# One mixture-of-experts block in two layers: token-major closing stage in layer 1, a token's expert rows side by side in DRAM

## The chip, the core and the metric

The kernel runs on one core of a Trainium2 chip. The metric is the device time in microseconds; the time shown is the median of three runs. The profile comes from one profiled execution, whose span stands a little below the time that it took.

## What is computed

Two layers of a hybrid token mixer and a mixture of experts over 512 latent and 256 context tokens of width D = 1024, all in float32. The second half of a layer and the last norm are what the change touches:

```python
def moe_ffn(h, router_w, router_b, e_gate, e_up, e_down, s_gate, s_up, s_down):
    scores = jax.nn.sigmoid((h @ router_w).astype(jnp.float32))
    _, idx = lax.top_k(scores + router_b.astype(jnp.float32), TOP_K)      # 6 of 64
    w = jnp.take_along_axis(scores, idx, axis=-1)
    w = (w / jnp.sum(w, axis=-1, keepdims=True) * ROUTED_SCALE).astype(h.dtype)
    return routed_experts(h, idx, w, e_gate, e_up, e_down) + swiglu(h, s_gate, s_up, s_down)
...
xl = xl + g1 * yl                                  # token mixer, gated
out = moe_ffn(hl2, ...)
xl = xl + g2 * out.reshape(b, n_lat, d)            # g2: one number per channel
...
return rms_norm(xl, final_norm_w)                  # after layer 1, latent tokens only
```

Layer 0 handles 768 tokens (six tiles of 128), layer 1 behind its mixer the 512 latent ones (four tiles).

## The kernel before

**Layout.** X, the residual stream, lies channel-major in SBUF: 128 channels on the partitions, eight chunks of channels, tokens along the free side. Nearly everything lives in one big SBUF tile, `arena`, through views, and the profile names it so. PSUM has eight banks of 128 x 512. Each engine has its own program; semaphores tie them. A table of jobs (`Plan`) gives each PSUM result its bank and says which engine reads it out ("A" for ACT, "D" for DVE); `start_job`, `ready` and `evacuated` are the waits that follow from it. A float32 product on TensorE shows as two records in the trace.

**Expert stage.** Each token goes to 6 of 64 experts. DVE, TensorE and POOL first build a table of slots (the index preparation: one-hot products, then `TG`, `TS` and `IXT`, L1926 to L1934). The work goes in blocks of 64 rows, in layer 1 with 11 blocks and eight experts to a round. Per block: POOL gathers rows from `hrows` (L2124); DVE turns them (`turn`, L1965); TensorE makes gate and up (L1062); ACT the silu (`gates`, L1442); DVE the hidden rows (`hidden`, L1972); TensorE turns those (L1070) and DVE copies them (`hidden_in`, L1977); TensorE makes the down product (L1084); ACT copies it out of PSUM into `YB` (`weighted`, L1450); POOL scatters `YB` to y in DRAM, 2 KB a row (L2132). SP streams the experts' weights, 3 MB each in two pieces (L530, L534). Partitions 0 to 63 of a down product hold channels 0 to 511 of 64 rows, partitions 64 to 127 channels 512 to 1023.

**y in DRAM.** Row (k, token, half), 512 numbers, lies at `(k * 1024 + token) * 2 + half`, k being which of the token's six experts made it.

**Closing stage of a layer.** SP waits for all scatters and then reads y back, a tile of 128 tokens in two halves of channels (L630), into a ring of three tiles, `Y6`; tile t waits until tile t - 3 is used. Meanwhile TensorE makes the shared expert's down products (L704, jobs `sd`) and DVE adds them to X, gated (`shared_added`, L1953). ACT scales three of a token's six rows (`weighted_rows`, L1475), DVE adds the other three, scaled (`sums`, L2027), TensorE turns and adds the three sums (L1128, jobs `ct`, 12 products over 128 columns a half), and DVE adds the result to X with the gate (`gated`, L2015). In layer 1 the last norm follows tile by tile: ACT squares (L1499), TensorE sums over channels (L1139, job `nf`), ACT takes the root (L1187), DVE the reciprocal (L1567) and eight products into H (`last_norm`, L2005), and SP stores the tile (L638) in pieces of 512 bytes, since the output is channel-major and turned on the host. In layer 0 ACT squares X for layer 1 (L1487) once tile 3 is gated.

The order in layer 1's closing is that of each engine's program:

```python
                    else:                                   # DVE, tile t, after sums(t)
                        if t:
                            last_norm(t - 1)
                        gated(t)
...
                        if t + 1 < pl.t_out:                # ACT, tile t
                            weighted_rows(t + 1)
                        for i in range(2):                  # then the squares of tile t
```

## Time and profile before

| what | value |
|---|---|
| median of 3 runs | 2374.71 us (2373.3 to 2379.6) |
| profiled execution: its time, its span | 2376.04 us, 2374.0 us |
| mean granted TensorE clock | 0.967 |
| busy share of the span: PE, DVE, ACT, POOL | 92%, 38%, 24%, 29% |
| chain that ended last, by engine | PE 73%, DMA 14%, DVE 8%, ACT 2% |
| transfers of y to SBUF (L630) | 20 of 1536 KB |
| expert loop of layer 0, of layer 1 | 675 to 1257 us, 1764 to 2310 us |
| closing stage of layer 0, of layer 1 | from 1257 us, 2310 to 2374 us |

A row of the timeline reads: start, duration, engine, line of the kernel, operation, output<-input, shape, count of the instructions merged into it, and in brackets the engine's idle time ahead of it with what ended that. Shares of busy time are averages over stages with different limits; what a change is worth is read in the stage that it touches. Where a DMA ends a wait, the DMA share of that window (1.00 and a little over is full) says whether more could have been moved.

### The profile page before, as it was taken

The page shows a single profiled execution, that of the slowest core. Times are in us where ns is not written, and L with a number is a line of the kernel's source. Part 1 is how long each engine was busy: PE and PEld are TensorE (multiplying, and loading weights), DVE is VectorE, ACT ScalarE, POOL GpSimd, SP SyncE. Part 2 cuts the span into 40 slices and gives each one's busy share as a digit, 9 for nine tenths or more (in the row PEclk, how much of TensorE's full clock was granted, in tenths as well). Part 3 has the DMA queues.
Part 4 walks back from the last instruction along what each step waited for, and adds up shares of the span by engine and source line. Part 5 has one row for each costly group of instructions (what it writes and reads, how often), then busy time and mean ns, then how long its engine had stood idle before and what let it go on. Part 6 is the DMA issues. An engine that isn't in the chain of part 4 may idle for free.

```text
span 2374.0 us, 36610 instructions
## 1 busy us (share of the span) xinstructions
PE 2180.4 (92%) x12802; PEld 1171.5 (49%) x12802; DVE 900.5 (38%) x1851; ACT 568.8 (24%) x1175; POOL 677.6 (29%) x811
## 2 busy tenths in 40 slices
PE   5998989898899999999998898899989999999897
PEld 1474344453645555555556463354445544455446
DVE  2295676312712222222226585663352121121117
ACT  4222154313201111111113522342211111111113
POOL 0000000000335555555551000000055554555530
PEclk8999989998799999999999999999999999999999
DMA  8612000363469999999987321000269999999977
GB/s 334 238 50 75 0 1 1 124 262 129 167 272 414 418 409 407 408 417 411 410 354 274 113 84 45 1 1 18 100 239 418 417 416 411 406 412 410 413 286 248
DMA packets 104856, 594.22 MB, mean 250 GB/s; under 512 B 25142, under 2 KB 29374, under 8 KB 62528
## 3 DMA queue, kind: packets, MB, share of 16 engines
q1 hardware_dynamic: 68656, 524.73, 54.8%
q0 software_dynamic: 34672, 63.07, 7.1%
q10 hardware_dynamic: 1440, 5.24, 0.5%
q8 instruction: 55, 0.90, 0.2%
q14 instruction: 33, 0.27, 0.0%
HBM read 572.95 MB, written 60.56 MB: 267 GB/s over the span
## 4 chain that ended last, share of the span: by engine, by line
PE 73%; DMA 14%; DVE 8%; ACT 2%; issue 2%; SPq 1%; DVEq 0%; ACTq 0%; POOLq 0%
PE psum L1062 23%; PE psum L704 19%; PE psum L1084 11%; DMA arena<-in_experts 11%; PE psum L870 3%; PE psum L894 2%; PE psum L910 2%; DMA arena<-in_mod_w 2%; PE psum L782 2%; PE psum L721 2%; PE psum L808 2%; PE psum L1070 2%; DVE arena L1567 1%; DMA arena<-y 1%; PE psum L1128 1%
## 5 line engine op out<-in xcount | busy, mean ns | idle before, releaser
L1062 PE MATMUL psum<-arena 128*64 128x256 f32 x6144 | 714.8, 386 | 33.9 <-DMA arena<-in_experts 26.8
L1062 PEld LDWEIGHTS psum<-arena 128*64 128x64 f32 x6144 | 438.1, 138 | 249.5 <-issue 40.8
L704 PE MATMUL psum<-arena 128*128 128x512 f32 (+1 forms) x1360 | 513.6, 534 | 20.0 <-DVE arena L1727 7.1
L2124 POOL DMA_INDIRECT arena<-hrows,IX x384 | 393.7, 1025 | 223.7 <-POOL IX L2116 156.9
L704 PEld LDWEIGHTS psum<-arena 128*128 128x128 f32 x1360 | 260.6, 195 | 262.5 <-issue 228.1
L1084 PE MATMUL psum<-arena 128*64 128x512 f32 x1536 | 364.8, 595 | 8.8 <-DMA arena<-in_experts 7.8
L1972 DVE TENSOR_TENSOR arena<-psum,arena 128x128 f32<-128x128 f32 x192 | 56.0, 292 | 606.5 <-ACT arena L1442 606.5
L2132 POOL DMA_INDIRECT y<-arena,IX x192 | 197.2, 1027 | 303.0 <-DVE arena L1965 198.7
L1442 ACT ACTIVATE arena<-psum 128x128 f32<-128x128 f32 x192 | 53.3, 278 | 673.1 <-PE psum L1062 673.1
L1450 ACT ACTIVATE arena<-psum 128x512 f32<-128x512 f32 x192 | 114.7, 597 | 312.1 <-PE psum L1084 312.1
L1084 PEld LDWEIGHTS psum<-arena 128*64 128x64 f32 x1536 | 112.4, 137 | 145.9 <-issue 120.9
L1977 DVE COPY arena<-psum 128x128 f32<-128x128 f32 x192 | 56.0, 292 | 271.9 <-PE psum L1070 271.9
L2083 POOL TENSOR_SCALAR arena<-con,arena 1x288 f32<-1x288 f32 x2 | 2.6, 1293 | 533.6 <-DVE arena L1858 533.6
L2074 POOL COPY arena<-arena 32x4608 f32<-32x4608 f32 x2 | 8.0, 4021 | 495.9 <-PE psum L808 495.9
L1965 DVE STREAM_TRANSPOSE arena<-arena 128x512 f32<-128x512 f32 x192 | 135.3, 705 | 11.3 <-DMA arena<-hrows,IX 7.1
L870 PE MATMUL psum<-arena 96*128 96x256 f32 (+1 forms) x288 | 104.1, 481 | 3.1 <-issue 3.1
L1070 PEld LDWEIGHTS psum<-con,arena 128*128 128x128 f32 x192 | 26.6, 139 | 157.8 <-issue 157.8
L1645 DVE SCALAR_TENSOR_TENSOR arena<-arena,par 128x512 f32<-128x512 f32 (+1 forms) x180 | 103.4, 650 | 0.0
L1349 ACT ACTIVATE arena<-psum,nm 128x768 f32<-128x768 f32 (+1 forms) x80 | 65.3, 816 | 112.1 <-DVE nm L1750 112.1
L1749 DVE TENSOR_REDUCE mx<-psum 128x1 f32<-128x768 f32 (+1 forms) x80 | 67.9, 849 | 34.8 <-PE psum L870 33.8
L910 PE MATMUL psum<-con,arena 128*128 128x128 f32 x416 | 62.3, 282 | 16.9 <-ACT arena L1370 9.4
L910 PEld LDWEIGHTS psum<-con,arena 128*128 128x128 f32 x416 | 44.9, 142 | 61.7 <-issue 34.5
(253 smaller groups left out, 1753.9 us busy)
## 6 DMA issues: line engine op xcount, KB each, us to landing
arena<-in_experts SPq DMA_DIRECT2D x128, 2048.0 KB, 19.1
arena<-in_experts SPq DMA_DIRECT2D x128, 1024.0 KB, 21.9
arena<-in_mod_w SPq DMA_DIRECT2D x48, 1024.0 KB, 8.1
arena<-y SPq DMA_DIRECT2D x20, 1536.0 KB, 15.4
arena<-in_wblk SPq DMA_DIRECT2D x22, 1024.0 KB, 4.9
arena<-in_shared SPq DMA_DIRECT2D x2, 3072.0 KB, 11.8
arena<-hrows,IX POOLq DMA_INDIRECT x384, 8.1
hrows<-arena ACTq DMA_DIRECT2D x10, 512.0 KB, 2.6
```

The source lines that it names most:

```text
L704: last = mm(job(l, key, n, parts), a, b, start=i == 0, stop=i == len(pairs) - 1)
L870: last = mm(flat[:, u % 2, i * LAT:i * LAT + n], QALL[0:QK, h, qt * P:(qt + 1) * P], KALL[0:QK, h, a:a + n], start=True, stop=True)
L910: last = nc.tensor.transpose(psum[:, bk, at * P:(at + 1) * P], PR[:, u % 2, i * P:(i + 1) * P], ident)
L1062: last = mm(psum[j * ROWS:(j + 1) * ROWS, (0, 1, 5)[u], 0:2 * P], HT[:, u, k, :], w[:, k * 512 + j * 256:k * 512 + (j + 1) * 256], start=k ...
L1070: nc.tensor.transpose(psum[:, 2, 0:P], HB[:, tour.third(s), :], ident).then_inc(sem(f"hid_T{l}"), 1)
L1084: last = mm(psum[q * ROWS:(q + 1) * ROWS, (3, 4, 6)[u], :], AT[:, u, j * ROWS:(j + 1) * ROWS], w[:, 4096 + j * D + q * 512:4096 + j * D + ...
L1450: f(YB[:, r, :], psum[:, (3, 4, 6)[tour.third(s)], :], ACT.Copy).then_inc(sem(f"y_a{l}"), 1)
L1645: op = V.scalar_tensor_tensor(dst, src, w, dst, ALU.mult, ALU.add)
L1749: link(V.reduce_max(mx[:, q], flat[:, u % 2, 0:n], AX))
L1965: V.transpose(HT[:, tour.third(s), :, :].rearrange("p k (t c) -> p t k c", t=2), GR[:, r, :]).then_inc(sem(f"turned{l}"), 1)
L2124: g.indirect_dma_start(GR[:, r, h * 256:(h + 1) * 256], None, rows, offsets(IX[:, s, h:h + 1]), bounds_check=4 * T * P - 1, oob_is_err=Fal ...
L2132: g.indirect_dma_start(y6d[l], offsets(IX[:, s, 2:3]), YB[:, r, :], None, bounds_check=TOPK * STRIDE * 2 - 1, oob_is_err=False).then_inc(s ...
```

## The change

1. **y's layout, both layers.** Row (token, half, k) now lies at `(token * 2 + half) * 8 + k`. A token's six rows of a half are 12 KB in one piece, and a transfer of y has 128 pieces of 12 KB instead of 768 of 2 KB. The last step of the index preparation computes these numbers (one instruction and one link of the chain more). The ring `Y6` is ordered by half first.
2. **The gate g2 goes into the experts' rows in layer 1.** A new job `gate` (8 small products) spreads g2 over the partitions; ACT copies it to `G2`. In layer 1 `weighted` moves from ACT to DVE and multiplies by `G2` instead of copying.
3. **Closing stage of layer 1, token-major.** TensorE turns X into PSUM with products against the identity (32 over 128 columns, into all eight banks: four tiles by two halves), then adds each half's three sums there with 3 products over 512 columns (jobs `xt`). DVE adds nothing to X behind the shared expert.
4. **The last norm, token-major.** A token is a partition, so ACT squares and sums a whole tile in one instruction (128 x 1024, accumulated) and takes a 128 x 1 root; DVE takes a 128 x 1 reciprocal and makes the output in two instructions of 128 x 512 from PSUM, with the norm's weights as rows in `FW`, 512 KB that SP loads ahead of the first transfer of y.
5. **The output** is stored token-major, 4 KB a piece.

```diff
@@ Plan
-            self.shared += ["signs", ("sg", 0, 0), "eid", ("sg", 1, 0)] + oh + ["tab", "ix", ("su", 0, 0), ("su", 1, 0)]
+            self.shared += ["gate", "signs", ("sg", 0, 0), "eid", ("sg", 1, 0)] + oh + ["tab", "ix", ("su", 0, 0), ("su", 1, 0)]
...
-            j += [(("ct", t, i), "D") for i in range(2)]
-            if l == LAYERS - 1:
-                j += [(("nf", t), "A")]
+            j += [(("ct" if l == 0 else "xt", t, i), "D") for i in range(2)]
...
+            elif k[0] == "xt":
+                bk = 2 * k[1] + k[2]
@@ SP
+                if l == LAYERS - 1:
+                    sp.dma_start(FW, A["final"]).then_inc(sem("final_in"), 16)
                 for t in range(pl.t_out):
                     if t >= 3:
-                        ready(sp, l, ("ct", t - 3, 1))
+                        ready(sp, l, ("ct" if l == 0 else "xt", t - 3, 1))
                     for i in range(2):
-                        half = slice(i * 512, (i + 1) * 512)
-                        sp.dma_start(Y6[:, t % 3, :, half], y6d[l].rearrange("(k t p c) d -> t p k c d", k=TOPK, p=P, c=2)[t][:, :, i, :]
+                        sp.dma_start(Y6[:, t % 3, i, :, :].rearrange("p k d -> p (k d)"),
+                                     y6d[l].rearrange("(t p c q) d -> t c p (q d)", p=P, c=2, q=8)[t, i, :, 0:TOPK * 512]
                                      ).then_inc(sem(f"y6in{t % 3}{i}"), 16)
...
-                sp.wait_ge(sem(f"norm_used{l}"), pl.norm[("nf", t)] + 1)
-                sp.dma_start(out[:, :, t * P:(t + 1) * P], H[:, :, t * P:(t + 1) * P]).then_inc(sem("out_done"), 16)
+                evacuated(sp, l, ("xt", t, 1))
+                sp.dma_start(out[t * P:(t + 1) * P, :], O[t]).then_inc(sem("out_done"), 16)
@@ TensorE
+                    elif st == "gate":
+                        start_job(st)
+                        for m in range(KC):
+                            q = m // 4
+                            last = mm(psum[q * ROWS:(q + 1) * ROWS, pl.bank[st], (m % 4) * P:(m % 4 + 1) * P],
+                                      modTs[l][:, 5 * KC + m, 0:1].to_broadcast([P, ROWS]), ident, start=True, stop=True)
+                        last.then_inc(done, 1)
...
+                if l == LAYERS - 1:
+                    evacuated(pe, l, ("sd", KC - 1, 0))
+                    for t in range(pl.t_out):
+                        for i in range(2):
+                            start_job(("xt", t, i))
+                            for k in range(4):
+                                mm(job(l, ("xt", t, i))[:, k * P:(k + 1) * P], X[:, 4 * i + k, t * P:(t + 1) * P], ident,
+                                   start=k == 0, stop=False)
+                    for t in range(pl.t_out):
+                        for i in range(2):
+                            pe.wait_ge(sem(f"ysum{l}"), 2 * t + i + 1)
+                            for y in range(3):
+                                last = mm(job(l, ("xt", t, i)), ident, Y6[:, t % 3, i, y, :], start=False, stop=y == 2)
+                            last.then_inc(done, 1)
@@ ACT
+                    elif st == "gate":
+                        ready(act, l, st)
+                        f(G2[:, :], job(l, st), ACT.Copy).then_inc(evacA, 1)
...
-                        weighted(s, i)
+                        if l == 0:
+                            weighted(s, i)
...
-                        for i in range(2):
-                            evacuated(act, l, ("ct", t, i))
...
-                        root(("nf", t), P)
+                        ready(act, l, ("xt", t, 1))
+                        f(JUNK, psum[:, 2 * t:2 * t + 2, :].rearrange("p b n -> p (b n)"), ACT.Square, accum_out=ssq[:, t:t + 1]
+                          ).then_inc(sem("sum_made"), 1)
+                        act.wait_ge(sem("sum_made"), t + 1)
+                        f(rms[:, t:t + 1], ssq[:, t:t + 1], ACT.Sqrt, bias=epsb[:, 0:1], scale=1.0 / D).then_inc(sem("rms"), 1)
@@ DVE
-                link(V.tensor_scalar(TS, job(l, "ix", 3 * SUBS)[:, 2 * SUBS:3 * SUBS], c("half"), None, ALU.add))
+                link(V.tensor_scalar(TS, job(l, "ix", 3 * SUBS)[:, 2 * SUBS:3 * SUBS], 0.5, -1.0, ALU.mult, ALU.add))
...
+                V.tensor_scalar(TU, TS, STRIDE - 1, 4, ALU.bitwise_and, ALU.logical_shift_left)
+                link(V.tensor_scalar(TS, TS, 10, None, ALU.arith_shift_right))
+                V.scalar_tensor_tensor(ixt[:, :, 2, :], TS.rearrange("p (h j) -> p h j", h=2), c("half"), TU.rearrange("p (h j) -> p h j", h=2),
+                                       ALU.add, ALU.add
...
+                def weighted(s, i):
+                    dve.wait_ge(sem(f"down{l}"), i * n + (s + 1))
+                    r, u = tour.place(s, tour.y_ring)
+                    dve.wait_ge(sem(f"scat{r}_{l}"), i * 16 * tour.uses(r, tour.y_ring) + (16 * u + scat0))
+                    dve.sem_inc(sem("passed"), 1)
+                    V.tensor_tensor(YB[:, r, :], psum[:, (3, 4, 6)[tour.third(s)], :], G2[:, :], ALU.mult).then_inc(sem(f"y_a{l}"), 1)
...
                             hidden(ahead, i * n + (s + 1))
+                        if l:
+                            weighted(s, i)
+                        if not (last_round and ahead == 0):
                             hidden_in(ahead, i * n + (s + 1))
...
                 def last_norm(t):
-                    r = recip(("nf", t), P)
-                    for k in range(KC):
-                        last = V.scalar_tensor_tensor(H[:, k, t * P:(t + 1) * P], X[:, k, t * P:(t + 1) * P], pr(l, "final", k), r,
-                                                      ALU.mult, ALU.mult)
-                    last.then_inc(norm_used, 1)
+                    dve.wait_ge(sem("rms"), t + 1)
+                    link(V.reciprocal(rms[:, t:t + 1], rms[:, t:t + 1]))
+                    if t == 0:
+                        dve.wait_ge(sem("final_in"), 16)
+                    for i in range(2):
+                        V.scalar_tensor_tensor(O[t][:, i * 512:(i + 1) * 512], job(l, ("xt", t, i)), rms[:, t:t + 1],
+                                               FW[:, i * 512:(i + 1) * 512], ALU.mult, ALU.mult).then_inc(evacD, 1)
...
-                    else:
-                        if t:
-                            last_norm(t - 1)
-                        gated(t)
-                evacuated(dve, l, ("ct", T - 1, 1))
+                    elif t:
+                        last_norm(t - 1)
```

**Where the order moves.** Line numbers of the changed kernel are its own. TensorE at the end of layer 1, from the last block's turned hidden rows on, before:

```order
L1070 MATMUL psum<-con,arena 128x128
L1084 MATMUL psum<-arena 64x512 x4
L704 MATMUL psum<-arena 128x512 x16
L1128 MATMUL psum<-con,arena 128x128 x24
L1139 MATMUL psum<-arena,con 128x128 x8
```

and now, L1133 being the products that carry X into PSUM and L1139 those that add the sums of y:

```order
L1084 MATMUL psum<-con,arena 128x128
L1098 MATMUL psum<-arena 64x512 x4
L711 MATMUL psum<-arena 128x512 x16
L1133 MATMUL psum<-con,arena 128x128 x32
L1139 MATMUL psum<-arena,con 128x512 x24
```

Before, the last two rows came once for each of the four tiles; now all 32 products of X stand ahead of the 24 that need y.

ACT at the same place, from the last copy of the experts' rows to the scaling of tile 2, before:

```order
L1450 ACTIVATE arena<-psum 128x512
L1475 ACTIVATE arena<-arena,WTS 128x512 x12
L1499 ACTIVATE arena<-arena 128x512 x2
L1187 ACT_TABLE_LOAD
L1187 ACTIVATE arena<-psum,epsb 128x128
L1475 ACTIVATE arena<-arena,WTS 128x512 x6
```

and now:

```order
L1461 ACTIVATE arena<-psum 128x128
L1495 ACTIVATE arena<-arena,WTS 128x512 x12
L1516 ACTIVATE arena,ssq<-psum 128x1024
L1519 ACT_TABLE_LOAD
L1519 ACTIVATE rms<-ssq,epsb 128x1
L1495 ACTIVATE arena<-arena,WTS 128x512 x6
```

The scaling of tile 2 (the last row) stands behind the square and the root of tile 0 as before, and these now wait for TensorE's products of tile 0 alone.

DVE, from the hidden rows of the last block on, before:

```order
L1972 TENSOR_TENSOR arena<-psum,arena 128x128
L1977 COPY arena<-psum 128x128
L1953 SCALAR_TENSOR_TENSOR arena<-psum,modT1,arena 128x512 x8
L2027 SCALAR_TENSOR_TENSOR arena<-arena,WTS 128x512 x6
L2015 SCALAR_TENSOR_TENSOR arena<-psum,modT1,arena 128x128 x8
```

and now, L2006 being the product with the gate row and L2062 the sums:

```order
L1993 TENSOR_TENSOR arena<-psum,arena 128x128
L2006 TENSOR_TENSOR arena<-psum,arena 128x512
L1998 COPY arena<-psum 128x128
L2004 REGISTER_ALU
L2006 TENSOR_TENSOR arena<-psum,arena 128x512
L1974 SCALAR_TENSOR_TENSOR arena<-psum,modT,arena 128x512 x8
L2062 SCALAR_TENSOR_TENSOR arena<-arena,WTS 128x512 x12
L2037 RECIPROCAL rms<-rms 128x1
L2041 SCALAR_TENSOR_TENSOR arena<-psum,rms,arena 128x512 x2
```

The gate product of a block stands between the next block's hidden rows and their copy, in every block of layer 1; in the closing the sums of tiles 0 and 1 follow each other, with nothing of tile 0 between them.

## Rows read from the trace of the kernel before

**Rows 1.** Windows: expert loops of layers 0 and 1, busy us by engine.

```profile
core 0: us, PE busy (x) PEld busy (x) DVE busy (x) ACT busy (x) POOL busy (x), PEclk, DMA share, GB/s
...
700.00:800.00 100.00, 100.00 (x738) 52.29 (x736) 21.80 (x54) 15.74 (x36) 58.90 (x72) 1.00 1.01 412
...
2190.00:2259.00 69.00, 62.98 (x453) 34.14 (x450) 13.34 (x33) 9.46 (x22) 35.77 (x45) 0.98 1.00 407
```

**Rows 2.** Timeline: layer 1's last blocks and closing stage.

```profile
2301.45 3.67 PE L1062 MATMUL psum<-arena 128*64 128x256 f32 x32
...
2307.58 1.94 PE L1084 MATMUL psum<-arena 128*64 128x512 f32 x8 [0.47 <-DVE arena L1977]
...
2310.63 13.97 PE L704 MATMUL psum<-arena 128*128 128x512 f32 x32 [1.12 <-ACT arena L1450]
...
2314.02 24.06 SPq L630 DMA_DIRECT2D arena<-y  x8
...
2324.64 0.75 DVE L1953 SCALAR_TENSOR_TENSOR arena<-psum,modT,arena 128x512 f32<-128x512 f32 x1 [0.97 <-PE psum L704]
...
2327.43 8.56 PE L1128 MATMUL psum<-con,arena 128*128 128x128 f32 x48 [2.83 <-DVE arena L2027]
...
2346.21 4.05 DVE L2027 SCALAR_TENSOR_TENSOR arena<-arena,WTS 128x512 f32<-128x512 f32 x6
...
2348.33 5.62 PE L1128 MATMUL psum<-con,arena 128*128 128x128 f32 x48 [0.16 <-DVE arena L2027]
...
2351.19 1.95 ACT L1475 ACTIVATE arena<-arena,WTS 128x512 f32<-128x512 f32 x3 [0.79 <-DMA arena<-y]
...
2353.27 2.15 DVE L2015 SCALAR_TENSOR_TENSOR arena<-psum,modT,arena 128x128 f32<-128x128 f32 x8
...
2359.31 0.95 DVE L1567 RECIPROCAL arena<-arena 128x128 f32<-128x128 f32 x1
...
2367.92 2.19 DVE L2005 SCALAR_TENSOR_TENSOR arena<-arena,par 128x128 f32<-128x128 f32 x8
```

**Rows 3.** Timeline: layer 0's closing stage.

```profile
1272.01 0.75 DVE L1953 SCALAR_TENSOR_TENSOR arena<-psum,modT,arena 128x512 f32<-128x512 f32 x1 [0.97 <-PE psum L704]
...
1278.19 3.22 DVE L1953 SCALAR_TENSOR_TENSOR arena<-psum,modT,arena 128x256 f32<-128x256 f32 x8
...
1307.27 1.95 ACT L1475 ACTIVATE arena<-arena,WTS 128x512 f32<-128x512 f32 x3 [2.12 <-DMA arena<-y]
...
1313.50 4.27 ACT L1487 ACTIVATE arena<-arena 128x512 f32<-128x512 f32 x8 [4.28 <-DVE arena L2015]
```

**Rows 4.** Windows: layer 0's closing, expert weights alone, layer 1's closing.

```profile
1295.00:1300.00 5.00, 3.65 (x30) 3.46 (x31) 4.24 (x12) 2.81 (x5) 0.00 (x0) 1.00 1.05 387
...
1745.00:1747.00 2.00, 1.68 (x30) 1.48 (x33) 0.23 (x1) 0.88 (x1) 0.00 (x0) 0.50 1.05 451
...
2328.00:2330.00 2.00, 2.00 (x12) 2.00 (x11) 0.60 (x1) 0.91 (x2) 0.00 (x0) 0.50 1.05 384
```

**Rows 5.** Instructions by form: count, busy us, mean ns, idle before.

```profile
L1450 ACT ACTIVATE arena<-psum 128x512 f32<-128x512 f32 x192 | 114.7, 597 | 312.1 <-PE psum L1084 312.1
...
L1349 ACT ACTIVATE arena<-psum,nm 128x768 f32<-128x768 f32 x64 | 57.7, 901 | 99.5 <-DVE nm L1750 99.5
...
L1802 DVE TENSOR_TENSOR arena<-psum,arena 128x512 f32<-128x512 f32 x4 | 2.8, 692 | 27.9 <-PE psum L704 26.6 <-issue 1.3
...
L1187 ACT ACT_TABLE_LOAD x5 | 6.4, 1283 | 0.1
```

**Rows 6.** Timeline: layer 1, where the gate row comes in.

```profile
1722.28 0.45 ACT L1422 ACTIVATE arena<-arena,con 128x192 f32<-128x192 f32 x1 [2.33 <-DVE arena L1858]
...
1728.25 0.81 PE L1011 MATMUL psum<-con,tot 128*1 128x128 f32 x6 [2.21 <-DVE tot L1891]
```

**Rows 7.** Timeline: layer 1 behind the index preparation.

```profile
1748.12 14.89 PE L704 MATMUL psum<-arena 128*128 128x512 f32 x32
...
1750.08 0.97 POOL L2116 COPY IX<-arena 128x3 int32 x2 [13.57 <-DVEq L1936]
...
1763.88 1.30 DVE L1965 STREAM_TRANSPOSE arena<-arena 128x512 f32<-128x512 f32 x2
```

53 lines of the change are left out of this document (22 added, 31 removed).

## The prediction

> **What bounds the kernel now.** I read four views: the windows of both expert loops, the timeline of each layer's closing stage, the windows of the same stretches, and the list of instruction forms for prices. The reader is to see three regimes.
>
> The expert loops. In layer 0 TensorE is busy 100.00 of 100 us while the DMA engines show a share of 1.01; in layer 1 TensorE is busy 62.98 of 69 us, the DMA share is 1.00 [rows 1]. Both loops therefore run at the DMA limit, and layer 1 waits for it. DVE is busy 21.8% and 19% there, ACT 16% and 14%. What the change puts on DVE in layer 1 has room; what it does to the transfers has none.
>
> The closing stage of layer 1, from the last down product to the end, 64 us. SP issues the eight transfers of y at 2314.02. ACT waits for them up to the last one, at 2351.19 (idle 0.79, released by the DMA) [rows 2]. Per tile of 128 tokens DVE works 4.05 (L2027, sums of the six rows), 2.15 (L2015, the gated addition to X), 0.95 (L1567, reciprocal) and 2.19 (L2005, final norm), 9.3 us. Two transfers take 2 x 4.07 = 8.14 us (the size and rate behind this stand below). So DVE sets the pace, and lags the last landing by 19 us: the last norm runs from 2367.92 to 2370.1, and the span ends at 2374.0 [rows 2].
>
> The closing stage of layer 0. ACT waits for y before nearly every half tile: one begins at 1307.27 after 2.12 of idle for the DMA. DVE needs only 4.1 + 2.15 = 6.3 us for a tile against 8.14 of transfer. The squares that open layer 1 start at 1313.50 [rows 3], after half (4,1). Transfers set this pace, at 387 GB/s with a share of 1.05 [rows 4].
>
> **The change, part by part.** The base is the profiled execution: span 2374.0, time 2376.0; the median of the runs is 2374.7, so I take gains off 2374.7.
>
> *Transfers of y.* A half tile is 128 x 3072 x 4 bytes = 1.573 MB, before as 768 pieces of 2 KB, now as 128 pieces of 12 KB. At 387 GB/s it takes 4.07 us. No transfer of y before has long pieces. Bounds: 387 GB/s (pieces don't matter) and 451 GB/s, the expert weights alone, whose pieces are 16 and 8 KB [rows 4]. I take 445, since the weights' row is the nearest in shape: 3.54 us, 0.53 saved.
>
> The Trainium skill (DMA: Bandwidth & Descriptors, "Why small descriptors are slow (HBM only)") states a fixed overhead of about 3 cycles for each packet beside its 32-byte beats; for 2 KB that is 3 in 67, an estimate of 4%. By it a half tile would still take 3.9 us and layer 0 would save 1.6 us where my sum has 5. The 451 against 387 GB/s of rows 4 is a larger step than that, so the trace speaks against the small figure.
>
> *Layer 0 closing.* Ten halves stand ahead of the squares: 10 x 0.53 = 5.3. Other engines cap it. DVE has shared additions up to 1272.01 + 0.75 = 1272.8 [rows 3] (the next eight begin at 1278.19 only because they stand behind the first sums), then 4.1 of sums, 3.2 of context additions, and for tiles 1 to 4 each 4.1 + 2.15, so gated tile 3 ends at 1305.7: at most 7.8 gained. And the transfers of tile 3 wait for TensorE's products of tile 0. Those follow 8 shared products over 256 columns and end at about 1284.6 (1279 + 24 x 0.234), just when the queue would run dry at 445 GB/s: a gap of at most 2 us, part of it behind DVE's own work. I take 5; bounds 0 and 7.8.
>
> *Layer 1, order.* Work falls away on DVE: 2.15, 0.95 and 2.19 a tile become a 128x1 reciprocal (about 0.2) and two 128x512 operations from PSUM (0.75 each by L1953). ACT loses two squares and a 128x128 root, gains one 128x1024 square from PSUM: 0.60 for 512 and 0.90 for 768 columns give some 1.15 [rows 5], and I allow 0.2 for reading its accumulator. TensorE: a product over 512 columns costs 13.97 / 16 = 0.873, one over 128 columns 5.62 / 24 = 0.234 (two records each) [rows 2]. So six new products a tile cost 5.24 (before 5.62 and 2.1), and 32 new ones carry X into PSUM: 7.5 us, once.
>
> Now the chain, from 2325.4, where DVE ends the last shared addition (L1953, 2324.64 + 0.75) [rows 2] and the 32 may start:
> X in PSUM 2332.9; tile 0 added 2338.1. ACT, in order, squares tile 0 (1.35), loads a table (1.28 [rows 5]), takes the root: 2341.3. Only then does it scale tile 2 (2 x 1.95): 2345.2; squares tile 1: 2347.0; scales tile 3: 2350.9. DVE's last sums and TensorE's (3,0), which holds (3,1) back by half a microsecond: products end at 2356.3. Then square 1.5 with hops, root 0.3, reciprocal 0.3, two outputs 1.6: 2360.1. The output takes 3.9 (2370.1 to 2374.0 before): 2364.0. **Gain 10.0.** The pace setter is a new one, ACT's queue behind TensorE's 7.5 us, not DVE and not y.
>
> Is y early enough? The transfers of tile 3 wait for ("xt", 0, 1), 2338.2, and land at 2343.8 and 2347.4; at 387 GB/s at 2345.9 and 2349.9. ACT takes them at 2347.0 and 2348.9, so the slow rate costs the tail 0.5 at most. FW (0.5 MB ahead of y on SP's queue) delays all landings by 1.2, hidden: the first sums wait for 2325.4 in any case. Bounds for the tail: 12.2 if ACT's order costs nothing and TensorE alone paces it (2325.4 + 7.5 + 4 x 5.24 = 2353.9, + 7.7); 7 if TensorE's clock stays low (below).
>
> *Expert loop of layer 1.* The 128x512 copy leaves ACT (0.597) and becomes a product on DVE (0.69 by the same form, L1802) [rows 5]. Behind it on DVE stands the copy of the next block's transposed hidden rows; TensorE wants that only after the next gate and up products, 3.67 us later [rows 2], so 0.69 is covered. POOL's scatter waits for it instead of for ACT: +0.1, covered. Where nothing covers it is the last block: there TensorE already waits 0.47 for that copy (L1084 at 2307.58 [rows 2]); it will wait 0.6 longer. **Loss 0.6**, bounds 0 and 1.
>
> *Gate row* (8 products of 128 columns, 1 us; one ACT copy 0.6): ahead of the signs in layer 1. TensorE waits 2.21 for the block numbers a little later, and ACT idles 2.33 just before the signs [rows 6]. Nothing; without that cover 1.6.
>
> *Index preparation*, both layers: one more shift-and-mask (0.3) and one link (0.3). POOL's first index copy goes from 1750.08 to 1750.7, while TensorE has 14.89 us of shared products from 1748.12 and DVE turns the first rows at 1763.88 [rows 7]. Nothing; layer 0 has two context passes more of the same cover.
>
> Sum: 5 + 10.0 - 0.6 = 14.4; 2374.7 - 14.4 = **2360.3**. What a measurement can tell from no change is 0.3%, 7 us.
>
> **Rivals.**
> A, the forecast, 0.55.
> B, pieces don't matter: y stays at 387 GB/s. For it: a share of 1.05 whatever the piece. Layer 0 gains nothing, the tail 9.5: 2374.7 - 9.5 + 0.6 = 2365.8. Chance 0.18.
> C, TensorE's clock. It fell to 0.50 (1.2 GHz) in 2328 to 2330 [rows 4], after 2.83 idle between the shared products and the first sums [rows 2]. With the 32 products there the idle shrinks to 2325.4 - 2324.6 = 0.8 us, so I expect the high level; at the low one for 6 us the chain starts 3 later: 2363.3. Chance 0.08.
> D, better: no gap in layer 0 (7.5) and ACT's order costs nothing (12.2), 512-byte pieces gone from the output (1): 2354.6. Chance 0.09.
> E, slower: the pitch. A token's rows now lie 32 KB apart, partition after partition, in reads and in the scatter. If lock-step streams collide, each of the 18 halves that count (10 and 8) grows. Price: 18 x 4.07 = 73 us per doubling. It decides from 13% on: 9.4 us of gain gone at 343 GB/s; by a quarter longer 2383. Against it: before, the six rows of a token lay 4 MB apart and ran at 387. The same would hit the scatters: of a round of 69 us the weights take 25.2 MB / 0.451 = 56, scatters and gathers 13; a fifth more on half of that is 1.3 us a round, eight rounds 10 us. Chance 0.06.
> The Trainium skill (DMA: Bandwidth & Descriptors, "Latency and other measured facts") names such a collision for row pitches that are large powers of two; its losses begin above 512 KiB, far over 32 KB, and no run here has shown one, so it does not raise the chance.
> F, DVE holds the loop: its product stands behind the turn of rows that may wait for a gather, so a late gather now delays scatter and PSUM release as well. Gathers are issued three blocks ahead, and a block is 3.67 + 1.94 us of products [rows 2]; a loss of 1 us a round would give 2368. Chance 0.04.
>
> **Numbers.** Likeliest 2360.3, printed as 2360. B gives 2366 and C on top of it 2368; D 2354 with a spread of 1 below. Range 2353 to 2368 leaves out E, part of F, and a little at either end, under 2 in 10. Faster by over 0.3% (below 2367.6): A, B, C, D, 0.90. Within: F and a mild E, 0.06. Slower: the rest, 0.04.
>
> **What would show it.** The windows of layer 0's closing at some 440 GB/s, not 387, and the squares of layer 1 at about 1308.5. In the tail: no 128x128 operations on DVE; 32 products from 2325 on for 7.5 us; ACT idle until tile 0's products end, then never waiting for the DMA; the last square about 15 us after the first. Rounds of layer 1 still 69 us apart and products of 0.69 on DVE. I am wrong if ACT still waits for y at the end, if the rounds lengthen, or if the tail gains under 7.

## The result, and the profile after

| | before | changed |
|---|---|---|
| median of the runs, us | 2374.97 (2369.44 to 2381.09, 8 runs) | 2358.0 (2352.49 to 2364.24, 8 runs) |
| ratio, 95% interval | | 0.9927 (0.9908 to 0.9946) |
| profiled execution, time and span, us | 2376.0, 2374.0 | 2353.7, 2352.0 |
| mean granted clock | 0.967 | 0.974 |

17.0 us faster; 14.4 were forecast. The profiled executions differ by 22.0. To see where, I cut each span at five rows that every kernel here has: the first gate product of a layer's expert loop, the last scatter of y that belongs to a block (POOL), the first squares of layer 1 (ACT), the end. All stage times below are differences of such starts.

| stage, us | before | changed | difference | forecast |
|---|---|---|---|---|
| start to expert loop of layer 0 | 674.88 | 671.92 | -2.96 | 0 |
| expert loop, layer 0 | 583.68 | 583.68 | 0 | 0 |
| closing of layer 0, to the squares | 54.94 | 50.51 | -4.43 | -5 |
| squares to expert loop of layer 1 | 451.20 | 448.15 | -3.05 | 0 |
| expert loop, layer 1 | 546.46 | 546.97 | +0.51 | +0.6 |
| tail, last scatter to the end | 62.84 | 50.77 | -12.07 | -10.0 |

The three stages that the change was meant to touch give 16.0. The other two, 6.0 together, are taken up with the experiments (run 11).

Windows of the changed kernel: both expert loops, then layer 0's closing stage (at its start and in its middle), then the tail.

```profile
core 0: us, PE busy (x) PEld busy (x) DVE busy (x) ACT busy (x) POOL busy (x), PEclk, DMA share, GB/s
700.00:800.00 100.00, 100.00 (x738) 52.26 (x736) 21.37 (x55) 15.64 (x36) 59.07 (x72) 1.00 1.01 413
2180.00:2249.00 69.00, 63.23 (x453) 34.27 (x449) 19.75 (x44) 3.05 (x11) 35.87 (x45) 0.98 1.00 407
1266.00:1268.00 2.00, 2.00 (x7) 0.80 (x6) 1.03 (x2) 0.34 (x1) 0.00 (x0) 1.00 1.03 424
1288.00:1293.00 5.00, 4.32 (x38) 4.13 (x38) 4.62 (x12) 3.13 (x5) 0.00 (x0) 1.00 1.00 424
2318.00:2322.00 4.00, 4.00 (x38) 4.00 (x38) 2.39 (x5) 1.95 (x3) 0.00 (x0) 1.00 1.02 433
```

Against [rows 1] the loops move the same bytes at the same share; in layer 1 a round's DVE work grew from 13.34 to 19.75 us and ACT's fell from 9.46 to 3.05, and the whole loop is 0.5 us longer. Against [rows 4], y comes at 424 to 433 GB/s and a share near 1.00, not at 387 and 1.05. The granted clock is 1.00 from the last scatter to the last product of the tail; before, it was 0.50 for some 6 us of it, while tile 0's products ran.

Timeline of layer 0's closing stage, changed kernel (ACT scales the landed rows, then opens layer 1).

```profile
1264.39 1.95 ACT L1495 ACTIVATE arena<-arena,WTS 128x512 f32<-128x512 f32 x3 [6.60 <-DMA arena<-y]
...
1288.14 1.95 ACT L1495 ACTIVATE arena<-arena,WTS 128x512 f32<-128x512 f32 x3 [1.75 <-DMA arena<-y]
...
1291.82 1.95 ACT L1495 ACTIVATE arena<-arena,WTS 128x512 f32<-128x512 f32 x3 [1.73 <-DMA arena<-y]
...
1299.88 1.95 ACT L1495 ACTIVATE arena<-arena,WTS 128x512 f32<-128x512 f32 x3 [1.75 <-DMA arena<-y]
...
1306.11 4.27 ACT L1507 ACTIVATE arena<-arena 128x512 f32<-128x512 f32 x8 [4.28 <-DVE arena L2050]
```

The same in the kernel before, beside the 1307.27 of [rows 3]:

```profile
1269.85 1.95 ACT L1475 ACTIVATE arena<-arena,WTS 128x512 f32<-128x512 f32 x3 [9.10 <-DMA arena<-y]
...
1303.20 1.95 ACT L1475 ACTIVATE arena<-arena,WTS 128x512 f32<-128x512 f32 x3 [2.12 <-DMA arena<-y]
```

At best ACT now starts halves 3.69 us apart (1284.44, 1288.14, 1291.82), before 4.07. It still waits for the DMA at each of the ten: transfers pace this stage as before, only faster. The gain comes in two parts. The first half lands 8.8 us after the last scatter (1255.60) and not 11.3 (1258.56), 2.5 sooner; from there to the last half it is 35.5 us and not 37.4, 1.9 less.

Timeline of layer 1's last block and of the tail, changed kernel.

```profile
2297.51 1.94 PE L1098 MATMUL psum<-arena 128*64 128x512 f32 x8 [0.96 <-DVE arena L1998]
...
2301.23 0.97 POOL L2166 DMA_INDIRECT y<-arena,IX  x1 [2.24 <-DVE arena L2006]
...
2311.66 1.95 ACT L1495 ACTIVATE arena<-arena,WTS 128x512 f32<-128x512 f32 x3 [16.76 <-DMA arena<-y]
...
2315.49 7.41 PE L1133 MATMUL psum<-con,arena 128*128 128x128 f32 x64 [0.84 <-DVE arena L1974]
...
2322.74 10.46 PE L1139 MATMUL psum<-arena,con 128*128 128x512 f32 x24
...
2328.09 1.02 ACT L1516 ACTIVATE arena<-psum 128x1024 f32<-128x1024 f32 x1 [3.41 <-PE psum L1139]
...
2329.22 1.28 ACT L1519 ACT_TABLE_LOAD   x1
...
2330.72 3.77 ACT L1495 ACTIVATE arena<-arena,WTS 128x512 f32<-128x512 f32 x6
...
2334.88 10.91 PE L1139 MATMUL psum<-arena,con 128*128 128x512 f32 x24 [1.68 <-DVE arena L2062]
...
2338.62 1.95 ACT L1495 ACTIVATE arena<-arena,WTS 128x512 f32<-128x512 f32 x3 [0.97 <-DMA arena<-y]
...
2345.83 1.02 ACT L1516 ACTIVATE arena<-psum 128x1024 f32<-128x1024 f32 x1 [3.93 <-PE psum L1139]
...
2347.50 1.41 DVE L2041 SCALAR_TENSOR_TENSOR arena<-psum,rms,arena 128x512 f32<-128x512 f32 x2
```

Up to the scaling of tile 2 (2330.72) the chain is the one forecast: X through TensorE (7.41), tile 0's products, square, table and root on ACT. The 0.97 at 2338.62 was not forecast: ACT does wait for the last half of y, and the rest of the tail follows from that landing.

### The profile page after: what moved, and what is told of

It is laid out like the page before. It is cut to its first block, busy times and chain, and to the rows that moved or that the text cites. A ratio compares the mean times of both kernels' runs of the same rounds, so it can differ in the third digit from the quotient of the medians.

```text
span 2352.0 us, 36281 instructions
## 1 busy us (share of the span) xinstructions
PE 2169.6 (92%) x12674; PEld 1154.9 (49%) x12674; DVE 940.0 (40%) x1887; ACT 516.1 (22%) x1088; POOL 679.0 (29%) x811
## 4 chain that ended last, share of the span: by engine, by line
PE 74%; DMA 12%; DVE 7%; issue 3%; ACT 2%; SPq 1%; DVEq 0%; ACTq 0%
PE psum L1076 24%; PE psum L711 19%; PE psum L1098 11%; DMA arena<-in_experts 10%; PE psum L877 3%; PE psum L901 2%; PE psum L917 2%; DMA arena<-in_mod_w 2%; PE psum L789 2%; PE psum L728 2%; PE psum L815 2%; PE psum L1084 2%; DVE arena L1585 1%; PE psum L830 1%; PE psum L1156 1%
## 5 line engine op out<-in xcount | busy, mean ns | idle before, releaser
L1986 DVE STREAM_TRANSPOSE arena<-arena 128x512 f32<-128x512 f32 x192 | 135.2, 705 | 26.9 <-DMA arena<-hrows,IX 19.9
L2006 DVE TENSOR_TENSOR arena<-psum,arena 128x512 f32<-128x512 f32 x88 | 60.9, 692 | 123.4 <-PE psum L1098 67.5
L1084 PEld LDWEIGHTS psum<-con,arena 128*128 128x128 f32 x192 | 26.6, 138 | 157.4 <-issue 157.4
L1469 ACT ACTIVATE arena<-psum 128x512 f32<-128x512 f32 x104 | 62.1, 597 | 162.6 <-issue 98.5
```

The lines of the kernel that those rows point to most:

```text
L1084: nc.tensor.transpose(psum[:, 2, 0:P], HB[:, tour.third(s), :], ident).then_inc(sem(f"hid_T{l}"), 1)
L1986: V.transpose(HT[:, tour.third(s), :, :].rearrange("p k (t c) -> p t k c", t=2), GR[:, r, :]).then_inc(sem(f"turned{l}"), 1)
```

## The experiments

Every kernel ran beside the kernel before on the same chip; the ratio is against it. Runs 1 to 4 were on one chip, 5, 6, 8 and 9 on a second, 7, 10 and 11 on a third, so kernels of different groups are compared by ratio and by stage. Stage times are from each one's profiled execution. The edits shown leave out what only follows from them (index numbers, views, semaphore counts).

| us | closing, layer 0 | loop, layer 1 | tail | span | median | ratio (95%) |
|---|---|---|---|---|---|---|
| before | 54.94 | 546.46 | 62.84 | 2374.0 | 2375.0 | |
| changed | 50.51 | 546.97 | 50.77 | 2352.0 | 2358.0 | 0.9927 (0.9908 to 0.9946) |
| 1 layout only | 50.34 | 546.18 | 61.37 | 2366.9 | 2366.6 | 0.9966 (0.9952 to 0.9981) |
| 2 closing only | 55.41 | 547.38 | 53.68 | 2363.4 | 2366.1 | 0.9966 (0.9955 to 0.9977) |
| 3 DVE takes the product | 55.12 | 547.61 | 62.64 | 2377.2 | 2377.9 | 1.0009 (0.9997 to 1.0022) |
| 4 early table | 50.43 | 547.34 | 50.91 | 2354.9 | 2357.0 | 0.9926 (0.9909 to 0.9942) |
| 5 four slots | 51.33 | 546.69 | 50.74 | 2360.6 | 2360.0 | 0.9929 (0.9905 to 0.9952) |
| 6 slots and table | 50.34 | 546.97 | 49.96 | 2351.7 | 2353.7 | 0.9908 (0.9889 to 0.9927) |
| 7 early weights | 50.41 | 548.03 | 50.79 | 2355.3 | 2360.0 | 0.9943 (0.9922 to 0.9963) |
| 8 pieces, wait misplaced | 50.09 | 549.20 | 61.41 | 2367.5 | 2368.6 | 0.9964 (0.9946 to 0.9981) |
| 9 pitch 24 KB | 50.70 | 547.41 | 50.83 | 2354.1 | 2360.2 | 0.9935 (0.9918 to 0.9952) |
| 10 pieces | 50.25 | 547.83 | 48.46 | 2350.6 | 2354.6 | 0.9917 (0.9901 to 0.9933) |
| 11 changed, again | 50.27 | 547.41 | 50.77 | 2352.9 | 2357.4 | 0.9929 (0.9913 to 0.9944) |

**1. The kernel before with the new order of y in DRAM only**, index preparation, scaling, sums and products fitted to it.

```diff
-    sp.dma_start(Y6[:, t % 3, :, half], y6d[l].rearrange("(k t p c) d -> t p k c d", ...)[t][:, :, i, :]
+    sp.dma_start(Y6[:, t % 3, i, :, :].rearrange("p k d -> p (k d)"),
+                 y6d[l].rearrange("(t p c q) d -> t c p (q d)", p=P, c=2, q=8)[t, i, :, 0:TOPK * 512]
```

> The kernel before with the new layout of y alone (pieces of 12 KB, the longer index preparation); gate, closing stage, norm and output as before. From the last scatter to the squares of layer 1 the kernel before takes 54.9 us (1258.56 to 1313.50) and the changed one 50.5 (1255.60 to 1306.11). If the pieces set the pace of layer 0's closing, this one takes 50.5 and its windows show about 428 GB/s; if the longer pieces gain nothing by themselves, 54.9 and 387. From the last scatter to the end of layer 1: before 62.8, changed 50.8. With DVE at 9.1 us a tile as the bound there, the layout alone gives at most 2 of the 12 us: 61 to 63. If transfers were the bound of that stage too, it would fall to some 58. In all 2368 to 2371 for a kernel before of 2375.

Layer 0 gets all of its gain from this (54.94 to 50.34). The tail gets only 1.5 of 12.1, to 61.37, inside the 61 to 63. The median, 2366.6, lies below the 2368 to 2371 expected. A window near the start of layer 0's closing in this run:

```profile
1266.00:1270.00 4.00, 4.00 (x10) 1.71 (x9) 2.08 (x3) 0.83 (x2) 2.26 (x3) 1.00 1.03 433
```

And its tail in the timeline, tile 0's products and two of the final norms:

```profile
2321.77 7.10 PE L1128 MATMUL psum<-con,arena 128*128 128x128 f32 x48 [2.83 <-DVE arena L2030]
...
2344.03 2.19 DVE L2008 SCALAR_TENSOR_TENSOR arena<-arena,par 128x128 f32<-128x128 f32 x8
...
2353.17 2.19 DVE L2008 SCALAR_TENSOR_TENSOR arena<-arena,par 128x128 f32<-128x128 f32 x8
```

The norms are still 9.1 us apart: faster transfers can't help where DVE paces. What the tail got, it got ahead of the first norm: tile 0's norm starts 29.4 us after the last scatter and not 30.9. In the kernel before, TensorE's 24 products of tile 0 (48 records) ran at the low clock and took 8.56 us [rows 2], here 7.10. That isn't where the 1.5 comes from, as run 3 shows below.

**2. The changed kernel with the old order of y in DRAM.**

```diff
-    sp.dma_start(Y6[:, t % 3, i, :, :].rearrange("p k d -> p (k d)"), ...
+    sp.dma_start(Y6[:, t % 3, i, :, :], y6d[l].rearrange("(k t p c) d -> t p k c d", ...)[t][:, :, i, :]
```

> The changed kernel with the old layout of y (768 pieces of 2 KB, old index preparation), everything else as changed. Layer 0's closing should be that of before: 54.9 us from the last scatter to the squares. For layer 1's closing the prediction said that the slow rate costs 0.5 at most (51.3 from the last scatter to the end where the changed kernel takes 50.8). The rival, from the changed kernel's trace, where ACT waits 0.97 for the last half: eight halves that are 0.38 us apart more cost about 3, so 53.5 to 54. In all 2362 to 2366 for a kernel before of 2375.

Tail 53.68, 9.2 under before and 2.9 over the changed kernel, as the rival of the expectation had it. Windows of layer 0's closing in this run, near the start and later:

```profile
1266.00:1270.00 4.00, 4.00 (x11) 1.75 (x10) 2.40 (x4) 0.00 (x0) 2.59 (x3) 1.00 0.88 262
...
1280.00:1290.00 10.00, 9.26 (x80) 9.13 (x79) 8.62 (x20) 4.94 (x8) 0.00 (x0) 1.00 1.05 386
```

And ACT's last three halves in the tail, from the timeline:

```profile
2342.17 1.95 ACT L1494 ACTIVATE arena<-arena,WTS 128x512 f32<-128x512 f32 x3 [1.03 <-DMA arena<-y]
...
2346.24 1.95 ACT L1494 ACTIVATE arena<-arena,WTS 128x512 f32<-128x512 f32 x3 [0.79 <-DMA arena<-y]
...
2350.25 1.95 ACT L1494 ACTIVATE arena<-arena,WTS 128x512 f32<-128x512 f32 x3 [2.06 <-DMA arena<-y]
```

Halves 4.0 to 4.1 us apart, each awaited. So in the token-major tail, with DVE's 9.3 us a tile gone, transfers of y are close behind ACT, and the two parts of the change help one another: 1.5 for the layout alone, 9.2 for the closing alone, 12.1 together, 1.4 more than the sum. The tails of one kernel repeat closely enough for that (50.77 twice for the changed one, 62.84 and 62.64 for the old closing in run 3). The ratios of whole runs can't show it: both are 0.9966, some 8 us with an interval of 3 either way.

**3. The kernel before with only the copy of a block's product moved to DVE in layer 1** (same YB and scatter; ACT's copy falls away).

```diff
@@ ACT
-                        weighted(s, i)
+                        if l == 0:
+                            weighted(s, i)
@@ DVE
...
+                    V.tensor_copy(YB[:, r, :], psum[:, (3, 4, 6)[tour.third(s)], :]).then_inc(sem(f"y_a{l}"), 1)
```

> The kernel before with only this moved: in layer 1 DVE instead of ACT takes the down product out of PSUM (a plain copy, no gate). From the first gate and up product to the last down product of layer 1: before 544.8 us, changed 545.2. Theory: the loop is held by transfers, the move costs 0.4 to 0.6 in the last block and nothing elsewhere, so 545 to 546 and 2375.5 in all. Rival F, DVE's queue holds up the loop: 4 us or more added to that stretch, rounds longer than 69.2.

The loop of layer 1 took 547.61, 1.15 more than before; in the other kernels that have this move it took 546.7 to 549.2 (the longest three are those that also load FW there), in the kernel of experiment 1, without it, 546.18. Some 0.5 of the difference is the last block, where TensorE's wait for the hidden rows is that of the changed kernel (timeline of this run):

```profile
2310.84 1.94 PE L1084 MATMUL psum<-arena 128*64 128x512 f32 x8 [0.96 <-DVE arena L1978]
```

before 0.47 [rows 2]. From the first gate product to the end of the last down product it is 545.8, inside the 545 to 546 expected. A loss of 1 us a round (rival F) would be over 7; there is none.

This run also has the old closing stage with y in the old order, and TensorE idles the same 2.83 us ahead of tile 0's products, but here the clock didn't fall (windows and timeline of this run):

```profile
2330.00:2336.00 6.00, 4.68 (x39) 4.50 (x40) 3.86 (x9) 3.56 (x6) 0.00 (x0) 1.00 1.05 386
...
2334.26 2.94 PE L1128 MATMUL psum<-con,arena 128*128 128x128 f32 x24 [0.51 <-DVE arena L2039]
```

Tile 0's products ended 22.6 us after the last scatter, not 24.8, and the tail was 62.64, 0.2 less than before. So the low clock cost the tail of the kernel before no more than some 0.2 us, and at least 1.3 of run 1's 1.5, where the clock fell too, come from the new order of y. And the 2.83 us of idle alone don't decide whether the clock falls.

**4. The changed kernel, the root's table loaded ahead of the first scaling.**

```diff
+                if l == LAYERS - 1:
+                    f(warm[:, 0:1], epsb[:, 0:1], ACT.Sqrt)
                 weighted_rows(0)
```

> The changed kernel with the table of the root loaded while ACT waits for the first y (a root of one column ahead of the closing stage). The chain that ended last goes through that table load (1.28 us) behind tile 0's square. If ACT's order alone holds the end, the closing stage from the last scatter to the end falls from 50.8 to 49.5. If the last transfer, which ACT waited 0.97 for, is tied with it, it falls by 0.5 at most, to 50.3.

Timeline of its tail:

```profile
2332.20 3.77 ACT L1495 ACTIVATE arena<-arena,WTS 128x512 f32<-128x512 f32 x6
...
2341.71 1.95 ACT L1495 ACTIVATE arena<-arena,WTS 128x512 f32<-128x512 f32 x3 [2.43 <-DMA arena<-y]
```

The scaling of tile 2 starts 1.3 us sooner after the last scatter (28.2 against 29.5), and ACT then waits 2.43 for the last half instead of 0.97. Tail 50.91, against 50.77: nothing. ACT and the last transfer are tied; taking time from ACT alone gives nothing.

**5 and 6. Four slots for landed rows in layer 1, without and with the early table.** Tile 3's transfers then wait for no product.

```diff
-                    if t >= 3:
-                        ready(sp, l, ("ct" if l == 0 else "xt", t - 3, 1))
+                    if t >= 3 and l == 0:
+                        ready(sp, l, ("ct", t - 3, 1))
...
-                        sp.dma_start(Y6[:, t % 3, i, :, :].rearrange("p k d -> p (k d)"),
+                        sp.dma_start(Y6[:, t % slots[l], i, :, :].rearrange("p k d -> p (k d)"),
```

> The changed kernel with four slots for the loaded token rows in layer 1 instead of three, so that tile 3's two transfers no longer wait for tile 0's products. If the transfers set the end of the tail: in the changed kernel the first half landed at 2311.66 and the last at 2338.6; eight halves 3.69 us apart would end at 2311.66 + 7 x 3.69 = 2337.5, so the last landing comes 1.1 us earlier and the tail is 49.7 us instead of 50.8. If ScalarE's own order (square and table between the scalings) sets it, the landing comes earlier and the tail stays at 50.8. Rate of the transfers 428 GB/s in both.

> As the run with four slots, and ScalarE's table for the square root is loaded before the first scaling of layer 1 instead of in the tail. Loading it early alone gained nothing (50.9 against 50.8). If transfers and ScalarE were tied, each hiding the other's gain, the two together give more than the sum of both: tail 49.2 us or less. If something third sets the end (VectorE's sums), the tail is as with four slots alone.

Four slots alone: 50.74, nothing. ACT's scaling of tiles 2 and 3 no longer waits for any DMA, but for its own square, table and root. Together: 49.96, 0.8 less, where 1.6 were expected. Timeline of the run with both:

```profile
2329.95 3.77 ACT L1496 ACTIVATE arena<-arena,WTS 128x512 f32<-128x512 f32 x6
...
2338.47 1.95 ACT L1496 ACTIVATE arena<-arena,WTS 128x512 f32<-128x512 f32 x3 [1.43 <-DMA arena<-y]
```

The last half now lands 36.7 us after the last scatter (37.4 in the changed kernel) and is the end of the wait again: eight halves at 3.69 us and FW ahead of them.

**7. The changed kernel, FW (0.5 MB) loaded during the experts' part.**

```diff
+                else:
+                    evacuated(sp, l, ("su", 1, 0))
+                    sp.dma_start(FW, A["final"]).then_inc(sem("final_in"), 16)
...
-                if l == LAYERS - 1:
-                    sp.dma_start(FW, A["final"]).then_inc(sem("final_in"), 16)
```

> The changed kernel with nothing altered but the place of the final weights' load (0.5 MB): during the experts' part instead of ahead of the token rows. The first landing comes 1.2 us earlier after the last scatter (9.2 instead of 10.4). If the end hangs on the landings alone: tail 49.6 us. If tile 3's transfers hang on tile 0's products, which start when TensorE is through with the products that carry X, the last landing does not move and the tail stays at 50.8.

Timeline, the first and the last half:

```profile
2313.32 1.94 ACT L1496 ACTIVATE arena<-arena,WTS 128x512 f32<-128x512 f32 x3 [15.15 <-DMA arena<-y]
...
2342.06 1.95 ACT L1496 ACTIVATE arena<-arena,WTS 128x512 f32<-128x512 f32 x3 [1.13 <-DMA arena<-y]
```

The last scatter was at 2304.51: the first half is 8.8 after it (10.4 in the changed kernel), the last 37.5 (37.4). Tail 50.79. Tile 0's products end 26.8 us after the last scatter in both kernels, and the last half lands some 10.7 us later in both: the last landing hangs on tile 0's products, as its second case had it.

**8 and 10. All of it together, and tile 3's halves in two transfers each** (rows 0 to 2 first), scaling, sums and products handed over row by row.

```diff
+    for q in range(2 if l and t == 3 else 1):
+        w = slice(q * 1536, (q + 1) * 1536) if l and t == 3 else slice(0, TOPK * 512)
...
                             for y in range(3):
+                                pe.wait_ge(sem(f"ysum{l}"), 3 * (2 * t + i) + y + 1)
```

> As the run with four slots and the early table, and: the final weights are loaded during the experts' part and not ahead of the token rows (0.5 MB at 428 GB/s: every landing 1.2 us earlier); tile 3's halves come in two transfers each, rows 0 to 2 first, so that ScalarE's 1.95 us of scaling runs while rows 3 to 5 land; and ScalarE, VectorE and TensorE hand over row by row. If the chain from the last landing over scaling, sum, products, square sets the end, as read in the changed kernel: tail 49.2 - 1.2 - 1.9 - about 0.7 = 45.4 us, span about 5 us under the changed kernel's at the same expert loops. If another engine sets it, over 48 us.

> Four slots, early table, early final weights, tile 3's halves in two transfers and hand-over row by row, as the run in pieces, but with the wait for tile 3's second pieces only ahead of tile 3's sums (it stood ahead of every tile's, which held VectorE until 2337). From the run with slots and table (tail 49.96, last landing 36.7 us after the last scatter): landing 1.2 earlier, ScalarE free for the last scaling at 35.3 after the scatter, its rows summed from 37.8 to 39.9, TensorE's products done 0.8 behind instead of 2.9: tail 47.0 us, 3.8 under the changed kernel. If VectorE's order sets it instead, 48.5 or more.

In run 8 the wait for tile 3's second pieces stood ahead of the sums of every tile, not of tile 3's alone. DVE stood still until they landed (timeline):

```profile
2337.02 2.08 DVE L2076 SCALAR_TENSOR_TENSOR arena<-arena,WTS 128x512 f32<-128x512 f32 x3 [16.73 <-DMA arena<-y]
```

and the tail was 61.41, 13 us over run 10. Most of it is the lost overlap of transfers and sums. A part is the clock: behind 10 us of idle TensorE ran the products that add the sums in part at the low clock and took 23.47 us for them, run 10 took 20.77. A window of run 8 shows that clock, and in the same row the rate of tile 3's halves in pieces of 6 KB:

```profile
2335.00:2337.00 2.00, 0.00 (x0) 0.00 (x0) 0.00 (x0) 0.00 (x0) 0.00 (x0) 0.50 1.02 421
```

Run 10, with the wait in its place: 48.46, 2.3 under the changed kernel, where 3.8 were expected. TensorE in its tail:

```profile
2301.58 13.97 PE L715 MATMUL psum<-arena 128*128 128x512 f32 x32 [1.23 <-DVE arena L2015]
...
2316.40 7.41 PE L1137 MATMUL psum<-con,arena 128*128 128x128 f32 x64 [0.84 <-DVE arena L1983]
...
2323.65 20.77 PE L1143 MATMUL psum<-arena,con 128*128 128x512 f32 x48
```

The 24 products that add the sums (48 records) run without a gap, right behind those that carry X, which take 7.25 up to their start: the tail is TensorE's now, 13.97 + 0.84 + 7.25 + 20.77 = 42.8 us to 2344.42, and 6.2 of square, root, norm and output after it. Neither of run 10's two theories had TensorE as the bound; run 8's "another engine" covers it.

**9. The changed kernel with tokens 24 KB apart in DRAM**, not 32.

```diff
-    y6d[l].rearrange("(t p c q) d -> t c p (q d)", p=P, c=2, q=8)[t, i, :, 0:TOPK * 512]
+    y6d[l].rearrange("(t p c q) d -> t c p (q d)", p=P, c=2, q=6)[t, i]
```

> The changed kernel with token rows 24 KB apart in DRAM (12 pieces of 2 KB a token, none left out) instead of 32 KB (16 pieces, 4 left empty). If a pitch that is a power of two costs the transfers nothing: windows of the closing stage of layer 0 at 424 to 433 GB/s as before, that stage 50.4 us, tail 50.8. If the power of two costs, as rival E had it: over 440 GB/s and halves 3.5 us apart instead of 3.69, layer 0's stage 48.9 us. The scatters in the expert loops are not expected to differ either way (loops 583.7 and 547.0 us).

Windows of layer 0's closing:

```profile
1264.00:1266.00 2.00, 2.00 (x6) 0.93 (x5) 0.75 (x1) 0.56 (x1) 0.97 (x1) 1.00 1.04 430
...
1270.00:1280.00 10.00, 10.00 (x63) 9.20 (x62) 10.00 (x19) 5.07 (x8) 0.00 (x0) 1.00 1.00 415
```

The changed kernel moves 418 GB/s in both of these windows; closing stage 50.70 and tail 50.83 against 50.51 and 50.77. Against 24 KB the pitch of 32 KB costs nothing.

**11. The changed kernel again.**

> The changed kernel once more, unaltered, on the same chip and in the same rounds as the two runs beside it, so that their times can be set against it. Tail 50.8 us, layer 0's closing stage 50.5, expert loops 583.7 and 547.0. What its span differs by from the first profile (2352.0) lies in the stretches ahead of the loops, where TensorE's granted clock differs from run to run; if it is within 1 us of 2352.0 with the same clock rows, the gap between the difference of spans (22.0) and of medians (17.0) is not luck of the clock.

Span 2352.9, within 1 of the first. By the criterion of the expectation the 22.0 would then not be luck of the clock, but the criterion was too weak: in both cases the profiled execution is one of the quick ones of its kernel (2353.7 where the median is 2358.0, here 2354.8 where it is 2357.4), while that of the kernel before was slightly slow (2376.0, median 2375.0). Of the 22.0 between the first two profiles, 6.0 lie in stages that the change hardly touches. A window some 140 to 180 us behind the squares, in the kernel before:

```profile
1450.00:1490.00 40.00, 32.73 (x96) 10.51 (x89) 24.60 (x31) 8.94 (x15) 0.00 (x0) 0.87 0.08 27
```

in the changed kernel:

```profile
1446.00:1486.00 40.00, 32.67 (x89) 10.19 (x86) 26.11 (x33) 8.34 (x14) 0.00 (x0) 1.00 0.08 27
```

and in the run with four slots:

```profile
1450.00:1490.00 40.00, 32.75 (x74) 10.13 (x72) 24.69 (x30) 8.34 (x14) 0.00 (x0) 0.87 0.08 27
```

The last number but two is the granted clock: 0.87, 1.00, 0.87. The run with four slots has the code of the changed kernel there, and needs 451.65 us from the squares to the loop, like the kernel before (451.20) and run 3 (451.00), which also shows the low clock there. The ten other profiles have 1.00 in this stretch: run 2 needed 446.36, the nine with the new index preparation 448.15 to 448.87. So TensorE's clock falls in that stretch in some executions, also of the changed kernel, and that is worth some 3 us; the 3.05 is not the change's. The 2.96 ahead of layer 0's loop may be of the same kind: runs 5 and 10 have the same code up to there and take 676.5 and 671.5. That is argued only; the four kernels with an old part take 674.9 to 677.2, the nine others 671.5 to 676.5.

All executions together say the same. The spans of 36 of the kernel before average 2373.2 us at a mean clock of 0.9694, those of 14 of the changed one 2355.8 at 0.9715. Within one kernel 0.001 less clock goes with 1.0 us more. At equal clock, an estimate from these executions, the change is then worth 15.2 us of the 17.4.

The change has one small price in that stretch, which two kernels at the same low clock show, the kernel before and the run with four slots (timeline, first gate product of layer 1's loop):

```profile
1764.70 3.67 PE L1062 MATMUL psum<-arena 128*64 128x256 f32 x32 [1.69 <-DVE arena L1965]
...
1763.17 3.67 PE L1077 MATMUL psum<-arena 128*64 128x256 f32 x32 [2.04 <-DVE arena L1987]
```

TensorE waits 1.69 in every profile with the old index preparation and 2.04 in every one with the new: the longer preparation isn't wholly covered in layer 1.

## Why the prediction was right

The forecast was 2360 and the median is 2358.0; by steps, 4.4 + 12.1 - 0.5 = 16.0 measured against 5 + 10.0 - 0.6 = 14.4. What bounds each stage was right; that the sum came so near is in part luck, since one term was too large and the other too small. One of the prediction's own signs of being wrong came true: ACT still waits for y at the end. The remaining 1.0 to the 17.0 of the medians is within what medians of one kernel differ by (2358.0 and 2357.4; before 2375.0 to 2376.3).

- *Bounds of the stages.* Right: transfers paced layer 0's closing (run 1 alone gives its gain, run 2 alone none), DVE paced the tail (with its norms still 9.1 us apart run 1 gave it 1.5; run 2, which takes that work away, 9.2). Run 2 changes the closing stage as a whole: no run shows what DVE's work, the norm and the output are worth each.
- *Transfers of y.* "I take 445" was too high: 415 to 433, at best 3.69 us a half. And the 4.4 of layer 0 isn't ten equal savings: 2.5 come from the first half, which lands that much sooner, and 1.9 from the nine behind it, whose steps average 3.94 (before 4.16), since two of them, 4.85 and 4.36, are longer at a DMA share near 1.00. At the start of the stage the old order of y runs at 262 GB/s in the very window in which run 1 shows 433 (some 5 to 10 us after the last scatter in both). The estimate by the Trainium skill (DMA: Bandwidth & Descriptors, "Why small descriptors are slow (HBM only)") was 3.9 us a half, from some 3 cycles for a packet; the measured step is about 10%, from 387 to about 428 GB/s, and the rule's is 4%. The measurement decides for the size of the step, but not for its cause. The new order makes the pieces longer and also brings together a token's six rows, which lay 4 MB apart; no run separates the two. The 6 KB pieces of run 8 still run at 421, and 12 KB pieces don't reach the 451 of the weights.
- *Layer 1's order.* Right in mechanism; place by place, after the last scatter (forecast, measured): tile 0 added 26.9 and 26.9; scaling of tile 2 begun 30.1 and 29.5; products' end 45.1 and 44.6; norms' end 48.9 and 47.7; end 52.8 and 50.8. Of the 2.1 us missed, 0.6 lie ahead of the products' end (ACT's square and hops; the wait of 0.97 for the last half is made up by shorter steps around it), 0.7 in the last square to norm (3.1, not 3.8), 0.8 in the output, which took 3.1 us and not "3.9". The last went to rival D and not into the sum. Small slips: the bound "at most 7.8" for layer 0 adds up to 8.4, the 12.2 for the tail to 12.4, and by the chain's own numbers the last square comes 18 us after the first, not "about 15" (measured 17.7). Nothing hangs on them.
- *"So the slow rate costs the tail 0.5 at most"* was wrong. Run 2 shows 2.9. It started tile 3's two transfers when tile 0's products release them, 27 us after the last scatter. At 4.07 us a half and with FW ahead, the queue is then still busy with tile 2: in run 2 that lands at 32.5 (2342.17), and tile 3's halves 4.07 and 8.1 later, at 40.5, not at the 38.7 of the step. The last scaling starts 3.1 later than in the changed kernel (40.5 against 37.4), and the end is 2.9 later. "Then never waiting for the DMA" was wrong with it: ACT waits 0.97. Had the new order not sped up y (rival B), the tail's gain would have been 9.2 and not 9.5; near enough, but by luck, since the 0.5 was 2.4 too small and the chain 2.1 too long.
- *Clock.* Rival C did not come: 1.00 up to the last product of the tail, with the idle ahead of the products that carry X at the forecast 0.8. That the short idle is the reason isn't shown, since run 3 kept 1.00 behind 2.83 of idle. Run 3 also shows that the low clock was worth only 0.2 in the kernel before, so avoiding it is no part of the gain to speak of.
- *Loop.* -0.5 for "loss 0.6", with the 0.96 in the last block as the place; in the second profile of the changed kernel (run 11) it is 0.95. The gate row is covered, as these rows of the changed kernel show beside [rows 6]:

```profile
1708.58 1.58 PE L1018 MATMUL psum<-con,modT 128*64 128x128 f32 x16
...
1717.79 0.82 PE L1025 MATMUL psum<-con,tot 128*1 128x128 f32 x6 [0.56 <-DVE tot L1909]
```

  TensorE's wait ahead of the block numbers shrank from 2.21 to 0.56.
- *Index preparation.* "Nothing" was wrong by 0.4 us in layer 1, the 2.04 against 1.69 above.
- *Rival E.* Excluded by run 9 for 32 against 24 KB. The Trainium skill (DMA: Bandwidth & Descriptors, "Latency and other measured facts") puts losses of power-of-two pitches above 512 KiB; this case agrees at 32 KB.
- *Rival F.* Run 3 leaves at most 1.2 to 1.4 us of 547 for it (against the kernel before and run 1), 0.5 of that in the last block.

The fastest versions are runs 6 and 10, with medians 2353.7 and 2354.6 against 2357.4 for the changed kernel. By the stage table their tails are 0.8 and 2.3 us shorter; the intervals of the ratios overlap, so that either beats the changed kernel as a whole is likely and not shown.
